# Out-projections of a hybrid encoder trunk in three passes of high and low halves

## What is computed

```python
h = rms_norm(x) * (1.0 + sc1) + sh1
y = mixer(h, w_in, ...) @ w_out            # o: (512, 1024), w_out: (1024, 1024)
x = x + g1 * y
h = rms_norm(x) * (1.0 + sc2) + sh2
x = x + g2 * hier_moe(h, ...)              # top-1 group, top-2 experts, w_gate_up and w_down of 32 experts
```

## Time and profile before

| What | Value |
|---|---|
| median of 3 runs | 1561.91 us (1560.99 to 1564.63) |
| the profiled execution's own time | 1555.12 us |
| its span | 1553.3 us |
| busy: TensorE, VectorE, ScalarE, GpSimd | 89%, 47%, 28%, 26% |
| mean granted TensorE clock | 0.941 |
| DMA over the span | 350.32 MB, mean 226 GB/s |

### The profile page before, as it was taken

The page is one execution under the profiler, slowest core; times in us unless marked ns, Lnnn a source line. Parts: engine busy times, 40 slices in busy tenths (PEclk is TensorE's granted clock), DMA queues, the critical chain, the costliest instruction groups (busy, mean ns, idle before and its releaser), DMA issues.

```text
span 1553.3 us, 25832 instructions
## 1 busy us (share of the span) xinstructions
PE 1381.2 (89%) x9273; PEld 920.9 (59%) x9273; DVE 726.1 (47%) x1526; ACT 434.3 (28%) x1017; POOL 406.1 (26%) x609
## 2 busy tenths in 40 slices
PE   4999998999999895999988599999999959999882
PEld 2877777677887554555544377677774445555440
DVE  3655555455655347632222424555555476422224
ACT  3334334244334210000000545555443110000002
POOL 3232022020223001343422333344430023434320
PEclk8899999999999996999989689999999969999996
DMA  8253553543015326999999503211117269999994
GB/s 357 91 214 130 200 200 127 196 166 119 10 55 216 96 91 242 415 423 422 420 422 418 215 21 117 82 68 68 68 68 311 82 241 372 419 422 422 423 401 193
DMA packets 56695, 350.32 MB, mean 226 GB/s; under 512 B 18408, under 2 KB 18880, under 8 KB 30992
## 3 DMA queue, kind: packets, MB, share of 16 engines
q1 hardware_dynamic: 44992, 332.02, 53.9%
q0 software_dynamic: 11520, 16.83, 3.0%
q10 hardware_dynamic: 80, 0.04, 0.0%
HBM read 342.45 MB, written 27.34 MB: 238 GB/s over the span
## 4 chain that ended last, share of the span: by engine, by line
PE 69%; DMA 18%; DVE 7%; ACT 3%; issue 2%; SPq 0%; ACTq 0%; POOL 0%; DVEq 0%; POOLq 0%
PE PS L989 8%; PE PS L746 7%; DMA hT<-in_moe_w_down_dram 7%; PE PS L748 7%; PE PS L747 7%; PE PS L937 6%; DMA Dr<-in_moe_w_down_dram 5%; DMA Dr<-in_ada_w_dram 4%; PE PS L996 4%; PE PS L829 3%; PE PS L848 3%; PE PS L717 3%; PE PS L845 2%; PE PS L1016 2%; PE PS L1006 2%
## 5 line engine op out<-in xcount | busy, mean ns | idle before, releaser
L746 PE MATMUL PS<-hHi,Whi 128*128 128x512 f32 x512 | 226.9, 443 | 3.7 <-issue 3.7
L1226 ACT COPY arena<-PS 128x512 f32<-128x512 f32 (+3 forms) x256 | 112.4, 458 | 332.2 <-PE PS L829 178.6
L748 PE MATMUL PS<-hHi,Wlo 128*128 128x512 f32 x512 | 202.5, 395 | 0.0
L747 PE MATMUL PS<-hLo,Whi 128*128 128x512 f32 x512 | 201.4, 393 | 0.0
L989 PE MATMUL PS<-Wr,arena 128*64 128x256 f32 x1408 | 167.1, 392 | 5.0 <-DVE arena L1998 4.8
L2207 POOL TENSOR_TENSOR Wlo<-Wr,Whi 128x512 fp32r<-128x512 f32 (+1 forms) x80 | 104.7, 1325 | 197.6 <-ACT Whi L1226 197.0
L989 PEld LDWEIGHTS PS<-Wr,arena 128*64 128x64 f32 x1408 | 102.5, 142 | 84.6 <-issue 31.5
L1432 ACT ACTIVATE arena<-PS 128x128 f32<-128x128 f32 x72 | 20.0, 277 | 472.2 <-PE PS L989 393.0
L2262 POOL DMA_INDIRECT y_rows<-arena x72 | 74.8, 1039 | 253.5 <-DVE arena L2010 240.8
L746 PEld LDWEIGHTS PS<-hHi,Whi 128*128 128x128 f32 x512 | 97.5, 190 | 35.3 <-issue 21.6
L748 PEld LDWEIGHTS PS<-hHi,Wlo 128*128 128x128 f32 x512 | 96.7, 189 | 21.9
(11 more groups left out here) (357 smaller groups left out, 2421.4 us busy)
## 6 DMA issues: line engine op xcount, KB each, us to landing
Wr<-in_moe_w_gate_up_dram SPq DMA_DIRECT2D x52, 2048.0 KB, 18.7
Dr<-in_ada_w_dram SPq DMA_DIRECT2D x42, 1024.0 KB, 26.7
Dr<-in_moe_w_down_dram SPq DMA_DIRECT2D x28, 1024.0 KB, 22.5
arena<-in_moe_w_gate_up_dram SPq DMA_DIRECT2D x14, 2048.0 KB
hT<-in_moe_w_down_dram SPq DMA_DIRECT2D x26, 1024.0 KB
Wr<-in_gdn_w_dram SPq DMA_DIRECT2D x8, 2048.0 KB, 8.6
Wr<-in_fox_w_dram SPq DMA_DIRECT2D x8, 2048.0 KB, 7.7
shift_scale<-in_moe_w_down_dram SPq DMA_DIRECT2D x12, 1024.0 KB
```

The lines of the kernel that those rows point to most:

```text
L746: mm(out_ap, a_hi, b_hi, start=(k == 0), stop=False)
L747: mm(out_ap, a_hi, b_lo, start=False, stop=False)
L748: return mm(out_ap, a_lo, b_hi, start=False, stop=(k == KD - 1))
L1226: return nc.scalar.copy(dst, src)
```

## The change

Both out-projections are made with `mm3`, like the input projections. The output weights are split into `Whi` and `Wlo` like a ninth and a tenth section: the first half in the head before the last, the second half in the last, by ScalarE with VectorE (layer 0) or GpSimd (layer 1). The mixer's result is split head by head: `out_hi` on ScalarE writes the high half to `outHi`, laid over `Dr`, and `out_lo` on VectorE writes the low half over `OT` itself. Since `Whi` now fills slots 2 and 3 of `Wr` and `outHi` fills `Dr` until the products are done, the loads of experts move: 3 and 4 behind unit 3, 0 with its down-weights behind unit 7, and 1, 2 and down-weights 1 behind the row stores.

```diff
+        outHi = sb_over(dr_at, "outHi", [P, KD, T])
...
+        outLo = sb_over(arena_at, "outLo", [P, KD, T])
...
                     load(X[:], x_rows.rearrange("(n p) d -> p n d", p=P), x_in)
-                for e in (0, 4):
-                    expert_load(layer, e, e)
...
-                for e in range(2):
-                    down_load(i, e, e)
                 sp.wait_ge(wo_ps, i * 2 * NT + NT)
-                expert_load(i, 3, 3)
+                for e in (3, 4):
+                    expert_load(i, e, e)
                 for n in range(NT):
                     sp.wait_ge(n_h, 4 * (2 * i + 1) + n + 1)
                     load(h_rows[i][n * P:n * P + P, :], hrow[n % 2], hr_out[n % 2])
                     if n == 1:
                         sp.wait_ge(wo_ps, (i + 1) * 2 * NT)
-                        expert_load(i, 1, 1)
-                        expert_load(i, 2, 2)
+                        expert_load(i, 0, 0)
+                        down_load(i, 0, 0)
+                for e in (1, 2):
+                    expert_load(i, e, e)
+                down_load(i, 1, 1)
...
+            def out_product(layer, nh, n, k):
+
+                pe.wait_ge(h_lo, (2 * layer + 1) * KD + k + 1)
+                if layer == 0:
+                    pe.wait_ge(w_lo, (H - 2 + nh) * KD + k + 1)
+                else:
+                    pe.wait_ge(w_lo_pool, (H + 2 + nh) * KD + k + 1)
+                return mm3(PS[(nh * NT + n) % 2][:], tile(outHi[:, k, :], n), tile(outLo[:, k, :], n),
+                           Whi[:, nh * KD + k, :], Wlo[:, nh * KD + k, :], k)
...
-                        mm(PS[u][:], tile(OT[:, k, :], u), Wr[:, 0, k, :], start=(k == 0), stop=False)
+                        out_product(layer, 0, u, k)
...
-                            last = mm(PS[u % 2][:], tile(OT[:, k, :], n), Wr[:, nh, k, :], start=(k == 0), stop=(k == KD - 1))
+                            last = out_product(layer, nh, n, k)
...
+            def out_hi(layer, h):
+
+                if layer == 0:
+                    act.wait_ge(ada_part, ADA_PER_HEAD * ADA_HEADS)
+                    act.wait_ge(ot_ok, h + 1)
+                else:
+                    act.wait_ge(on_ok, h + 1)
+                at = ds(h, 1)
+                cp(outHi[:, at, :], OT[:, at, :]).then_inc(h_hi, 1)
...
                         weights_hi(par, PIECES[l])
+                    if 2 < l < 3 + len(heads):
+                        out_hi(0, heads[l - 3])
...
-            step(6, 0, 4)
-            step(7, 1)
-            delta(7, None, lambda m: None, 1)
+            step(6, 0, 4, (0, 1, 2))
+            step(7, 1, 5, (3, 4, 5))
+            delta(7, None, lambda m: None, 1, 5, (6,))
             head_norm(7)
+            out_hi(0, 7)
...
                         weights_hi(par, (2 * qt,))
+                    if qt == 0 and (not isinstance(p, int) or p > 0):
+                        out_hi(1, p - 1)
...
-            pair_step(7, 1)
-            attend(7, lambda m: None, 1)
+            pair_step(7, 1, 5)
+            attend(7, lambda m: None, 1, 5)
+            out_hi(1, 7)
...
+            def out_lo(layer, h):
+
+                dve.wait_ge(h_hi, h + ((2 * layer + 1) * KD + 1))
+                at = ds(h, 1)
+                TT(outLo[:, at, :], OT[:, at, :], outHi[:, at, :], ALU.subtract).then_inc(h_lo, 1)
...
+                    if 2 < l < 3 + len(heads):
+                        out_lo(0, heads[l - 3])
+                    for k in PIECES[l]:
...
                         TS(pS[a][:, 0:w], pS[a][:, 0:w], rinv[:, u:u + 1], None, ALU.mult).then_inc(pn_ok, 1)
+                    if qt == 0 and (not isinstance(p, int) or p > 0):
+                        out_lo(1, p - 1)
...
-                if split:
-                    weights_lo(p % 2, p * KD + (H + 2) * KD)
+                weights_lo(p % 2, p * KD + (H + 4) * KD)
```

More of the change, by code:

```diff
@@ L884, in delta, with out_part @@
                 mm(PS[6][:], ones[:], osq, start=True, stop=True).then_inc(sso_ps, 1)
-            def out_part(layer, w_sem, ready, fills):
+            def out_product(layer, nh, n, k):
[6 more added lines that the diff above has]
+                           Whi[:, nh * KD + k, :], Wlo[:, nh * KD + k, :], k)
+            def out_part(layer, fills):
                 def fill(a, b):
@@ L918, in _, with out_projection @@
             step(7, 1)
-            delta(H - 1, out_part(0, mix_w, ot_ok, 4 * KD), 1, more=False)
-            def out_projection(layer, w_sem, ready, ready_n):
+            delta(H - 1, out_part(0, 4 * KD), 1, more=False)
+            def out_projection(layer):
                 pe.wait_ge(modq_in, 32 * (layer + 1))
@@ L1323, in take_product, with delta @@
                 cp(cin[m % 2][:, CONV - 1:], PS[m % 2][:]).then_inc(ev_pj, 1)
-            def delta(d, s, take, par, w_n=None):
+            def out_hi(layer, h):
[6 more added lines that the diff above has]
+                cp(outHi[:, at, :], OT[:, at, :]).then_inc(h_hi, 1)
+            def delta(d, s, take, par, w_n=None, heads=()):
                 act.wait_ge(k_ps, d + 1)
@@ L1395, in ada_item, with step @@
                     act.dma_start(ada_rows[ds(d * 2 + (2 + i), 1)].rearrange("a j c -> (a j) c"), ada_acc[0:97:32, i, :]).then_inc(ada_out[i], 16)
-            def step(s, slot, w_n=None):
-                delta(s - 1, s, lambda m: take_product(s, m), (slot + 1) % 2, w_n)
+            def step(s, slot, w_n=None, heads=()):
+                delta(s - 1, s, lambda m: take_product(s, m), (slot + 1) % 2, w_n, heads)
             for m in range(3):
@@ L1742, in delta @@
                         TT(t4(vb), t4(PS[3][:]), over(irk), ALU.mult).then_inc(vb_ok, 1)
-                    for k in PIECES[l] if split else ():
+                    if 2 < l < 3 + len(heads):
+                        out_lo(0, heads[l - 3])
+                    for k in PIECES[l]:
                         dve.wait_ge(w_hi, d * KD + (2 * KD + k + 1))
@@ L1775, in _ @@
                 link.leave(2)
-            delta(H - 3, H - 2, 1)
-            delta(H - 2, H - 1, 0, split=False)
-            delta(H - 1, None, 1, split=False)
+            delta(H - 3, H - 2, 1, (0, 1, 2))
+            delta(H - 2, H - 1, 0, (3, 4, 5))
+            delta(H - 1, None, 1, (6,))
             head_out(H - 1, 1)
+            out_lo(0, H - 1)
             def out_projection(layer):
@@ L2153, in _ @@
                 link.leave(H - 1)
+            out_lo(1, H - 1)
             out_projection(1)
@@ L2378, in attend @@
                     last.then_inc(cbt_ok, 1)
-                if split:
-                    weights_lo(p % 2, p * KD + (H + 2) * KD)
-            weights_lo(1, (H + 1) * KD)
+                weights_lo(p % 2, p * KD + (H + 4) * KD)
+            weights_lo(1, (H + 3) * KD)
             attend(0)
-            with pool.Fori(1, H - 2) as p:
+            with pool.Fori(1, H) as p:
                 attend(p)
-            for p in range(H - 2, H):
-                attend(p, split=False)
             experts(1)
```

26 lines of the change are left out of this document (10 added, 16 removed).

## The result

| | before | after |
|---|---|---|
| median | 1561.1 us (20 runs, 1552.96 to 1568.74) | 1566.95 us (20 runs, 1558.65 to 1573.02) |
| the profiled execution: own time, span | 1555.12, 1553.3 us | 1567.37, 1565.6 us |
| mean granted clock | 0.941 | 0.932 |

The ratio is 1.0037, 95% interval 1.0020 to 1.0055: the change costs 5.8 us, where 7.9 us of gain were forecast. The forecast's sign is wrong, and the result lies outside its range.

What follows compares the result with a forecast made beforehand. TensorE (69% of the chain) was taken to bound the kernel, DMA the expert stage. Layer 0's -5.45 and layer 1's -2.45 gave -7.9 us, 1561.9 to 1554.0; own range 1549 to 1559, over the cases 1545.5 to 1564.5.

Steps and rivals of the forecast that it cites:

- Layer 1's last pair: Layer 1's last pair, splitting half 1: +1.0 us for ScalarE's load wait, +1.0 for GpSimd's subtractions; +2.0 together, bounds 0 and +5.
- Products: Out-projection units 2 to 7: 0.180 us less per product, -8.6 us a layer, +0.3 for float32 switches.
- Splitting in layer 0: Casts and subtractions for weights and heads in layer 0's last heads fit into idle time: 0, bound above 2 us.
- Fills: TensorE's fills in the last head or pair get shorter: -0.8 us in layer 0, -0.3 in layer 1.
- the sign of being wrong that the prediction gave for this head: Last head: the forecast is wrong if the granted clock falls below 1.00 within it.
- The start: Between last head and unit 2: +0.65 us later start and +0.3 for the clock in layer 0, +0.45 in layer 1.
- Pairs 1 to 6: Layer 1's pairs, where `out_hi` and `out_lo` delay the next scores: +1.0 us for six pairs, bounds 0 and +9.9.
- Rival C: `out_lo` blocks VectorE by 1.65 us in each of six pairs, last pair pays 4; sum +3.0, 1564.9 us; chance 0.12.
- rival D: The clock falls in `delta(7)` or the last pair, 20 us of matmuls at the lower clock; 1574 us; chance 0.07.
- The gather: First gather of each expert stage shares DMA with moved loads: +2.7 us a layer, bounds 0 and +5.5.
- Rival B: The first gather waits until the load queue drains, 7.4 us a layer; 1563.4 us, no measurable change; chance 0.15.

Runs made afterwards that it cites:

- run 1: The changed kernel with SyncE loading half 0 of layer 1's output weights ahead of the last pair's bias rows; 1557.48 us, ratio 0.9991 to the kernel before.
- run 11: Repeat of run 5: the changed kernel with half 0 loaded first and three down-weights held behind each first gather; 1549.19 us, ratio 0.9936.
- run 6: Run 5 plus useless matmuls ahead of the first out-projection product, three in layer 0 and one in layer 1; 1545.52 us, ratio 0.9905.
- run 8: The changed kernel with the edits of run 5, run 6 and run 7 together; 1548.77 us, ratio 0.9925.
- run 12: Run 6 plus two more useless matmuls in layer 1's last pair, where TensorE waits for the first scaled scores; 1546.15 us, ratio 0.9922.
- run 4: The changed kernel with half 1 of layer 1's output weights split after the last pair instead of in it; 1576.01 us, ratio 1.0117.
- run 7: Run 5 with ScalarE's wait for half 1 and TensorE's wait for the mixer's low half moved later; 1549.49 us, ratio 0.9929.
- run 2: The changed kernel with down-weights 4, 2 and 3 issued only after each expert stage's first gather has landed; 1563.36 us, ratio 1.0023.
- run 9: The changed kernel with nothing edited, measured again beside run 10 and run 11; 1565.93 us, ratio 1.0032.
- run 10: Repeat of run 2: the changed kernel with three down-weights held behind each first gather; 1559.58 us, ratio 0.9994.
- run 3: The kernel before, with float32 products and no splitting, only its expert loads moved as in the change; 1569.85 us, ratio 1.0061.
- run 5: The changed kernel with the edits of run 1 and run 2 together; 1548.47 us, ratio 0.9924.

## Why the prediction was wrong

**The failed step is a term taken as nothing: the wait for half 0 in pair 6.** Under "Layer 1's last pair" the prediction asked when the load for the newly split half lands, and found +1.0. It asked that for half 1 only. Half 0 is split a pair earlier, and its load was taken to come as the other pairs' loads do. Its row was on the table: the earlier trace rows show the first of the two issued at 1142.75, and the same timeline has the bias row 0.39 us ahead of it, at 1142.36, behind GpSimd's masks. Landing 7.9 us later, it would be there at 1150.7, while ScalarE's first exponential of pair 6 stood at 1143.80 in that trace. That is 6.9 us, read off three numbers. The prediction's own method gives the loss from these rows; it was applied to one of two loads. In after the load landed at 1155.6, the wait grew by 7.9 us, and the low clock behind it made the stage 9.2 us longer. Run 1 shows that this is all of the stage's loss, and 7 us of time.

**Products: right.** 5.2 us for 32 products a layer in units 4 to 7, 0.164 each against the forecast 0.180 less the float32 switches.

**Splitting in layer 0: right.** 0 was taken, and heads 5 and 6 kept their lengths.

**Fills: right, but not in the profile after.** -0.8 was taken for layer 0. From `X`'s issue to head 7's result it took 48.5 us before and 48.9 after, +0.4. In nine of the twelve profiles with the split it takes 47.4 to 47.7, which is the -0.8 and a little more. The other three (after, runs 1 and 11) take 48.9 to 49.0, and these are the ones in which the clock falls in this head. So the sign of being wrong that the prediction gave for this head, a clock under 1.00, came true in some executions, at 1.2 us each.

**The start: mis-sized in layer 0.** +0.65 and +0.3 for the clock were taken. Unit 2 started 1.0 later behind the result, and units 2 and 3 took 12.45 instead of 14.03 us, 1.3 less gain than at full clock. With the clock held (runs 6, 8, 12) the stretch from head 7's result to unit 3's end is 15.7 us, against 17.8 before: -2.1, where -1.9 was forecast for it. It is 17.2 in after and 16.1 in runs 4 and 11, which have the same products. So the clock's term was mis-sized, and its size changes from execution to execution. In layer 1 the start cost 0.1 instead of 0.45.

**Pairs 1 to 6: right, and better than that.** +1.0 was taken; it was 0 (run 1). Rival C, 6 x 1.65, fell, though its mechanism is real. VectorE's groups of `outLo`, by form:

```profile
L1731 DVE TENSOR_TENSOR outLo<-arena,outHi x7 | 10.4, 1487 | 10.5 <-ACT outHi L1232 10.5
L1731 DVE TENSOR_TENSOR outLo<-arena,outHi 128x512 fp32r<-128x512 f32 x9 | 6.2, 686 | 1.4 <-ACT outHi L1232 1.4
```

Seven of the sixteen, those beside GpSimd's subtractions, take 1.49 us instead of 0.69, behind a wait of 1.5 us for ScalarE, and TensorE's projection products cover it.

**The last pair: right place, half the size, and the wrong causes.** +2.0 less 0.3 was taken, +3.3 was measured. The prediction named the load's wait and GpSimd's subtractions beside VectorE, 1.0 each. Run 7 takes the first away and gains nothing; run 4 has neither, and its pair is as long as that of runs 1, 2, 9 and 10. Run 12 shows that 2.2 of after's 3.3 were rival D's mechanism, the clock, which the prediction priced at nothing in its sum and gave 0.07 as a case of 20 us. Most of the rest goes with the masks, which it didn't name. That something else lengthened the very pair that the prediction named is luck.

**The gather: right mechanism, mis-sized.** +2.7 a layer was taken, +3.9 and +3.2 were measured, nearer the 8.5 us of the full stage than the middle between that and 3.0. Rival B, 7.4 a layer, fell: the gather would have landed some 10 us after its start, 3 us behind the last load, and it landed after 7.0, while the engines were still full. By the Trainium skill (DMA: Bandwidth & Descriptors, section on queues, rings and completion order) each engine alternates between the queues that have work; the trace agrees as far as the gather did not wait for the loads to end. But it landed only some 1 us (layer 0) and 2 us (layer 1) before the engines emptied, so what it would take beside a longer queue isn't shown here. Runs 2 and 3 show the cause, loads beside the gather, from both sides.

Put together, the terms that were named come to -7.9 forecast and, by the table, to -2.8 (expert stages left out); pair 6 adds the 9.2 that turn it over. With half 0 first and the down-weights held, the change is worth 12 and 10 us in runs 5 and 11 (ratios 0.9924 and 0.9936), where the forecast without its price for the gather says 13.3, inside both intervals. With matmuls of no use it is 15, 12 and 12 (runs 6, 8 and 12); that these gain time over runs 5 and 11 isn't resolved.

## What to carry to other kernels

When a step that used a steady pattern in a loop gets one more round behind the loop, read the queue's order at the loop's end again: a load that was early for its old reader can be late for its new one, without its issue having moved. Do it for every load whose first reader changes, not only for the last. A stretch with slack for a microsecond of waiting on TensorE may have none for its clock: look at what TensorE does there, and where a wait can't go, useless matmuls in it are a cheap trial (here 3 us in the stages of run 6, and a gain in time too small to be resolved). And before a wait or a neighbour is blamed for a longer stage, take it out: run 4 took out both suspects of the last pair, and its length stayed.

## What the runs showed of the hardware

GpSimd's back-to-back subtractions slowed small VectorE operations by what a whole subtraction takes, whatever their own size: 1.22 us each for operations of 0.16 (run 4). Two engines' work that fits side by side by its busy shares doesn't fit by that count.

TensorE's granted clock went from 1.00 to 0.50 (2.4 to 1.2 GHz) around one wait of 1.8 us and a shorter one between two short transposes, in a stage that is otherwise dense. In the eleven profiles with this wait the fall came between 0.7 us before and 2.1 us after its end, and the clock was down for some 3.5 to 7 us. It stayed at 1.00 when the wait was filled (run 12), and in the kernel before, where the wait is 0.84 us. The same kernel's clock fell at a place in one execution and not in another (head 7: after, but not run 9). The Trainium skill (TensorE: Matmul & The Clock Gate, Part 1) says that activity releases the throttle and idleness brings it back; the trace agrees, 0.57 against 1.00 with and without the wait.
